# A two-block transformer kernel: the second mixer's attention regrouped into units of four heads, with half of the output mix placed between them

## The reference

```python
# first block, one layer
mix = (jax.nn.sigmoid(gate_a) * (nsa_out @ w_proj_a[layer])
       + jax.nn.sigmoid(gate_b) * (ret_out @ w_proj_b[layer]))
...
# second mixer, fox branch: 8 heads of 64, causal, with a forget term F per head
s = jnp.einsum('bqhd,bkhd->bhqk', qb, k) * scale
s = s + Fq[..., None] - F[:, :, None, :]
s = jnp.where(mask[None, None], s, -jnp.inf)
p = jax.nn.softmax(s, axis=-1)
...
# second mixer, dsa branch: an index score picks 128 keys of each query
score = jnp.einsum('bqh,bqhk->bqk', iwb, jax.nn.relu(dots))
_, sel = lax.top_k(score, top_k)
...
merged = jax.nn.sigmoid(ga) * (ya @ w_br_fox) + jax.nn.sigmoid(gb) * (yb @ w_br_dsa)
return merged @ w_out
```

## Time and profile before

| what | us |
|---|---|
| median of 3 runs | 2283.05 (2280.05 to 2284.55) |
| the profiled execution, its own time | 2287.16 |
| its span, first to last instruction | 2285.1 |
| PE busy | 2159.1 |
| DVE, ACT, POOL busy | 942.5, 768.4, 796.9 |

### The profile page before, as it was taken

How to read it: one execution, slowest core, us unless ns; L and a number is a source line. 1 busy time by engine, 2 the same in 40 slices (tenths; PEclk the granted TensorE clock), 3 DMA queues, 4 the chain that set the end, 5 groups by cost and what they waited for, 6 DMA issues and landing times.

```text
span 2285.1 us, 26992 instructions
## 1 busy us (share of the span) xinstructions
PE 2159.1 (94%) x9858; PEld 1684.8 (74%) x9858; DVE 942.5 (41%) x1403; ACT 768.4 (34%) x1321; POOL 796.9 (35%) x333
## 2 busy tenths in 40 slices
PE   5997799999999999799999989999899998999999
PEld 4777455587778888688788877745567887888887
DVE  6662544432662353546711136637842124110110
ACT  3332355533332332323232244334353224221221
POOL 2363311134354354234444423300002442444442
PEclk8998899999999999799999989958699999999999
DMA  5344111134567457336434422210002342334332
GB/s 137 97 117 106 27 47 38 32 83 111 138 175 207 125 157 209 103 101 176 124 84 100 102 71 68 67 26 1 1 1 56 84 110 65 93 100 105 88 92 74
DMA packets 156810, 211.22 MB, mean 92 GB/s; under 512 B 15240, under 2 KB 133416, under 8 KB 156584
## 3 DMA queue, kind: packets, MB, share of 16 engines
q1 hardware_dynamic: 140128, 166.24, 29.2%
q10 hardware_dynamic: 16584, 43.64, 6.3%
HBM read 206.69 MB, written 2.10 MB: 91 GB/s over the span
## 4 chain that ended last, share of the span: by engine, by line
PE 79%; DVE 9%; issue 6%; ACT 3%; POOL 2%; ACTq 1%; DMA 1%; DVEq 0%; POOLq 0%
PE ps L611 23%; PE ps L613 22%; PE ps L612 22%; PE ps L980 2%; POOL wlo L575 2%; PE ps L1002 2%; PE ps L1014 1%; PE ps L856 1%; PE ps L885 1%; DVE top L2092 1%; DVE score L2095 1%; PE ps L842 1%; PE ps L872 1%; DVE xT L2129 1%; PE ps L861 1%
## 5 line engine op out<-in xcount | busy, mean ns | idle before, releaser
L575 POOL TENSOR_TENSOR wlo<-raw,whi 128x1024 fp32r<-128x1024 f32 (+1 forms) x317 | 781.4, 2480 | 1443.4 <-ACT whi L1280 1426.2
L611 PE MATMUL ps<-hhi,whi 128*128 128x512 f32 x1488 | 596.9, 401 | 14.3 <-DVE hlo L1778 7.4
L613 PE MATMUL ps<-hhi,wlo 128*128 128x512 f32 x1488 | 585.3, 393 | 0.0
L612 PE MATMUL ps<-hlo,whi 128*128 128x512 f32 x1488 | 585.3, 393 | 0.0
L1280 ACT ACTIVATE whi<-raw 128x1024 fp32r<-128x1024 f32 x309 | 315.9, 1053 | 408.1 <-PE ps L613 401.8
L611 PEld LDWEIGHTS ps<-hhi,whi 128*128 128x128 f32 x1488 | 282.7, 190 | 86.7 <-issue 20.5
L613 PEld LDWEIGHTS ps<-hhi,wlo 128*128 128x128 f32 x1488 | 282.8, 190 | 60.2
L612 PEld LDWEIGHTS ps<-hlo,whi 128*128 128x128 f32 x1488 | 283.6, 191 | 56.7 <-issue 1.4
L611 PE MATMUL ps<-hidhi,whi 128*128 (+1 forms) x608 | 236.9, 390 | 3.0 <-DVE mod L2150 3.0
L613 PE MATMUL ps<-hidhi,wlo 128*128 (+1 forms) x608 | 236.6, 389 | 0.0
L612 PE MATMUL ps<-hidlo,whi 128*128 (+1 forms) x608 | 236.5, 389 | 0.0
(11 more groups left out here) (324 smaller groups left out, 2743.3 us busy)
## 6 DMA issues: line engine op xcount, KB each, us to landing
raw<-in_ffn_w SPq DMA_DIRECT2D x264, 256.0 KB, 3.8
raw<-in_w_in SPq DMA_DIRECT2D x154, 256.0 KB, 4.0
trig<-in_ada_w ACTq DMA_DIRECT2D x72, 512.0 KB, 4.3
raw<-in_w_up SPq DMA_DIRECT2D x64, 256.0 KB, 3.9
raw<-in_w_down SPq DMA_DIRECT2D x64, 256.0 KB, 3.8
raw<-in_w_out SPq DMA_DIRECT2D x32, 256.0 KB, 3.7
xrow<-in_x ACTq DMA_DIRECT2D x2, 1024.0 KB, 10.0
raw<-in_cmp_k_w SPq DMA_DIRECT2D x8, 256.0 KB, 3.9
```

Source lines behind the costliest of these rows:

```text
L575: last = pool.tensor_tensor(lo, src, hi.bitcast(F32), ALU.subtract)
L611: pe.matmul(out_, lhi, rhi, start=first, stop=False)
L612: pe.matmul(out_, lhi, rlo, start=False, stop=False)
L613: return pe.matmul(out_, llo, rhi, start=False, stop=last)
```

## The change

Four things are rebuilt. (1) fox and dsa become 16 units of four heads (`UNITS2`: fox blocks 3, 3, 2, 2, 1, 1, 0, 0, then dsa 0, 0, 1, 1, 2, 2, 3, 3) in 18 rounds, in the form of `nsa_attention`: paired scores, all masks and the forget term added by PE (the forget row `FThl` in two fp32r parts on 8 + 8 partitions, picked by `selr`), maxima straight from PSUM, one `normalise` per unit, `transpose` in place of a product with a diagonal. The index products become 10 units of two or four heads, blocks 1, 2, 3, on two PSUM banks, and the selection runs in the order 1, 2, 3 by the table `SELECTED`. (2) The fox branch of the output mix (`mixa2`, 12 slabs) runs in rounds 8 to 16 by the table `FILL2`; the dsa branch (`mixb2`, 12 slabs) follows the attention. (3) The gates of the interleaved branches are Tanh of half the input in place of Sigmoid; the branch sum is taken with (1 + tanh), and halved later. (4) The first norm squares rows of x (`xrow`, now loaded in four tiles of 128 whole rows) on ACT with accumulation along the row; constants are loaded in three pieces; SP's slabs from the second on wait for x; ACT rounds slab 0 between the squares, slab 1 after the vectors, and slabs 2 and 3 after the `hhi` chunks.

```diff
+        UNITS2 = [("fox", i, cc) for i in reversed(range(NT)) for cc in range(2)]
+        UNITS2 += [("dsa", i, cc) for i in range(NT) for cc in range(2)]
+        BLOCKS2 = [i + 1 for _, i, _ in UNITS2]
+        TURNS2 = [sum(BLOCKS2[:u]) for u in range(len(UNITS2) + 1)]
+        FILL2 = [0] * 9 + [2, 4, 7, 10, 13, 16, 19, 22, 24, 24]
...
-        SELECT_AT = [(12, 21), (22, 28), (28, 34)]
...
+        SELECTED = [0, 0, 4, 12, 20, 27, 34, 40, 46, 57, 68, 78, 88, 96, 102, 102, 102, 102, 102]
...
+                if s == 1:
+                    for t in range(NT):
+                        sp.wait_ge(ld_x[t], 16)
...
-            def attention(ph):
-                steps = STEPS[ph]
-
-                def scores(s):
-                    t = steps[s]
-                    n, i = t["n"], t["i"]
-                    if s >= 3:
-                        pe.wait_ge(at_exp[ph], s - 2)
-                    mask = {"causal": (i * P, C_CAUSAL, P), "fox": (i * P, C_CAUSAL, P), "cmp": (0, C_CMP + 32 * i, n),
-                            "dsa": None}[t["mask"]]
-                    mm = pe.matmul(ps[:, s % 3, 0:n], t["q"], t["k"], start=True, stop=mask is None)
-                    if mask is not None:
-                        at, c, w = mask
-                        mm = pe.matmul(ps[:, s % 3, at:at + w], ident, cst[:, c:c + w], start=False, stop=True)
-                    mm.then_inc(at_qk[ph], 1)
...
-                def turn(s):
-
-                    t = steps[s]
-                    pe.wait_ge(at_nrm[ph], s + 1)
-                    if s >= 2:
-                        pe.wait_ge(at_pt[ph], s - 1)
-                    for j in range(len(t["v"])):
-                        nk = min(P, t["n"] - j * P)
-                        mm = pe.matmul(ps[0:nk, 3 + s % 2, j * P:j * P + P], PB4[s % 4][:, j * P:j * P + nk], diag[:, s % 2, :],
-                                       start=True, stop=True)
-                    mm.then_inc(at_tr[ph], 1)
...
+            def fd_attention():
+
+                def score_pair(u, p):
+                    kind, i, cc = UNITS2[u]
+                    n, c, x = (i + 1) * P, 2 * cc + p, 4 * u + 2 * p
+                    if x >= 2:
+                        pe.wait_ge(at_exp["fd"], x - 1)
+                    for g in range(2):
+                        rows_ = slice(64 * g, 64 * g + 64)
+                        q, k = (fqT, fkT[rows_, c, 0:n]) if kind == "fox" else (dqT, dkT[rows_, 0, 0:n])
+                        pe.matmul(ps[:, (x + g) % 3, 0:n], q[rows_, c, i * P:(i + 1) * P], k, start=True, stop=False)
+                    if x == 0:
+                        pe.wait_ge(f_ready, 1)
+                    if kind == "dsa" and cc == 0 and p == 0:
+                        pe.wait_ge(ix_sel, i + 1)
+                    for g in range(2):
+                        bank = ps[:, (x + g) % 3, :]
+                        if kind == "fox":
+                            h = 2 * c + g
+                            pe.matmul(bank[:, 0:n], selr[:, h:h + 1].broadcast_to([P, P]), FThl[:, 0:n], start=False,
+                                      stop=False)
+                            mm = pe.matmul(bank[:, i * P:n], cstr[:, 0, :], cstr[:, 1, :], start=False, stop=True)
+                        else:
+                            mm = pe.matmul(bank[:, 0:n], cstr[:, 0, :], sel[:, i, 0:n], start=False, stop=True)
+                        mm.then_inc(at_qk["fd"], 1)
...
+                    for p in range(2):
+                        for g in range(2):
+                            mm = pe.transpose(ps[:, 3 + t % 2, (2 * g + p) * P:(2 * g + p + 1) * P],
+                                              P3[u % 3][:, 2 * p + g, j * P:j * P + P], ident)
+                    mm.then_inc(at_tr["fd"], 1)
...
+                    if kind == "fox":
+                        for p in range(2):
+                            for g in range(2):
+                                c = 2 * cc + p
+                                v = fv[:, j, 64 * (2 * c + g):64 * (2 * c + g) + 64]
+                                mm = pe.matmul(ps[64 * g:64 * g + 64, 5, P * c:P * c + P], v,
+                                               SQ[t % 4][:, P * (2 * g + p):P * (2 * g + p) + P], start=j == 0 and p == 0,
+                                               stop=j == i, skip_group_check=True)
+                    else:
+                        for g in range(2):
+                            mm = pe.matmul(ps[64 * g:64 * g + 64, 5, 256 * cc:256 * cc + 256], dvrow[:, j, :],
+                                           SQ[t % 4][:, 256 * g:256 * g + 256], start=j == 0, stop=j == i)
+                    mm.then_inc(at_pv["fd"], 1)
+
+                def filler(r, a, b):
+                    for q in range(4 * FILL2[r] + a, 4 * FILL2[r] + b):
+                        branch("mixa2", q // 4, q % 4, q % 4 + 1, O2["a"], (at_done["fd"], NT))
+
+                n = len(UNITS2)
+                for r in range(n + 2):
+                    nb = BLOCKS2[r - 2] if r >= 2 else 0
...
+                    for j in range(nb + 1):
+                        if j == (nb + 1) // 2:
+                            if 2 * r + 1 < len(UNITS):
+                                index_unit(2 * r + 1)
+                            if r < n:
+                                score_pair(r, 1)
+                        if j < nb:
+                            turn(r - 2, j)
+                        filler(r, quarters * j // (nb + 1), quarters * (j + 1) // (nb + 1))
+                        if j >= 1:
+                            values(r - 2, j - 1)
...
                 if n == 0:
+                    sc.wait_ge(ld_misc, 16)
+                    sc.activation(early[:, 0:1], col(C_EPS), ACT.Sqrt)
+                    for t in range(NT):
+                        if t == 2:
+                            high(0)
+                        sc.wait_ge(ld_x[t], 16)
+                        sc.activation((st, tmp)[t // 2][:, 2 * (t % 2):2 * (t % 2) + 2, :].rearrange("p a n -> p (a n)"), xrow[:, t, :],
+                                      ACT.Square, accum_out=early[:, 1 + t:2 + t]).then_inc(x_summed, 1)
+                    sc.wait_ge(x_summed, NT)
+                    sc.activation(root[:, 0, :], early[:, 1:1 + NT], ACT.Sqrt, bias=col(C_EPS), scale=1.0 / D).then_inc(n_root, 1)
+                    for m in (7, 6, 5, 4):
+                        sc.wait_ge(x_turned, KD - m)
+                        sc.activation(xT[:, m, :], ps[:, m, :], ACT.Copy).then_inc(x_ready, 1)
                     sc.wait_ge(vec_turned, 1)
                     sc.activation(vec[:, :], ps[:, 2, 0:P], ACT.Copy).then_inc(vec_ready, 1)
                     sc.wait_ge(vec_turned, 2)
                     sc.activation(vec2[:, :], ps[:, 3, 0:V2_N], ACT.Copy).then_inc(vec_ready, 1)
...
-                        if r % 6 == 3:
-                            for c in range(2):
-                                sc.wait_ge(*one_done(mb_g, "mixb1", r // 6, c, 2))
-                                if r >= 6:
-                                    sc.wait_ge(mb_m, 2 * (r // 6 - 1) + c + 1)
-                                sc.activation(gsig[:, c, :], ps[:, 6 + c, :], ACT.Sigmoid).then_inc(mb_sig, 1)
+                        if r % 6 in (2, 3):
+                            c = r % 6 - 2
+                            sc.wait_ge(*one_done(mb_g, "mixb1", r // 6, c, 2))
+                            if r >= 6:
+                                sc.wait_ge(mb_m, 2 * (r // 6 - 1) + c + 1)
+                            sc.activation(gsig[:, c, :], ps[:, 6 + c, :], ACT.Tanh, scale=0.5).then_inc(mb_sig, 1)
...
+                def filled(r):
+                    for d in range(FILL2[r], FILL2[r + 1]):
+                        n, step, c = d // 6, d % 6 // 2, d % 2
+                        if c == 1:
+                            high(AT["mixa2"] + d // 2 + SLOTS)
+                        if step == 1:
+                            sc.wait_ge(*one_done(mb_g, "mixa2", n, c, 2))
+                            if n >= 1:
+                                sc.wait_ge(mb_m, 8 + 2 * (n - 1) + c + 1)
+                            sc.activation(gsig2[:, c, :], ps[:, 6 + c, :], ACT.Tanh, scale=0.5).then_inc(mb_sig, 1)
...
-            for half in range(2):
-                cols = slice(half * D // 2, (half + 1) * D // 2)
-                sc.dma_start(xrow[:, :, cols], T["x"][0].rearrange("(t p) d -> p t d", p=P)[:, :, cols])\
-                  .then_inc(ld_x[half], 16)
+            sc.dma_start(cst[:, 0:C_HD128], T["consts"][:, 0:C_HD128]).then_inc(ld_cst, 16)
+            for t in range(NT):
+                sc.dma_start(xrow[:, t, :], T["x"][0, t * P:(t + 1) * P, :]).then_inc(ld_x[t], 16)
+            with nc.allow_non_contiguous_dma(reason="9 narrow columns"):
+                sc.dma_start(cst[:, C_MISC:C_END], T["consts"][:, C_MISC:C_END]).then_inc(ld_misc, 16)
...
+            def fd_attention():
+
+                def maxima(u, p):
...
```

(30 more changed lines are left out.)

656 lines of the change are left out of this document (254 added, 402 removed), and 2 rows, old and new, of the table C_END.

## The result

The changed kernel took 2157.7 us (median of 4 runs, 2156.4 to 2160.5) against 2283.8 us before (4 runs): a ratio of 0.945, 95% interval 0.943 to 0.947. The forecast was 2166. The profiled execution took 2156.66 us, its span is 2154.6.

What follows compares the result with a forecast made beforehand. PE, busy 2159.1 of 2285.1 us, was taken as the bound. Gains of 99.7 (attention), 6 (gates) and 11 (start), 116.7 off 2287.2, gave 2170.5; 2166 after allowing for that execution lying 4.1 above the median; range 2140 to 2202.

Steps and rivals of the forecast that it cites:

- the likeliest case: Whole kernel: full clock in fox rounds 2 to 4 and from round 8 on; 2166 us, chance 0.48.
- rival B: Second mixer's attention: clock stays full in the fox part, 12 us less, 2154 us; chance 0.17.
- the fox term: Rounds 0 to 7 of the second mixer's attention: 70 us with losses plus 12 for the clock, 82 us.
- the clock: Fox rounds 0, 1 and 5 to 7 at half clock because PE waits there: 11.4 us, 12 with the 5%.
- the larger engine of each round: Rounds 0 to 17: the longer of PE and DVE summed, 66.7 and 113.5 us, plus 5% for losses.
- fox values: Fox rounds, PE: four products of 128 columns per block, taken at 0.80 us, between 0.58 and 1.01.
- Rival A: Fox part stays at half clock to round 7, PE the longer, 104 us against 82: 2188 us; chance 0.22.
- Dsa rounds: Rounds 8 to 17, with the fox branch's twelve slabs: 113.5 us plus 5%, 119 to 119.5 us.
- the collision: DVE and POOL excluding each other in rounds 8 to 16: 1 to 3 us, inside the 5%.
- Gates: First mixer's attention: no table loads at four gates, PE's waits shrink; gain 6 us, from 0 to 8.
- Start: First norm: first product at 26 instead of 37.41, gain 11 us, from 6 to 15.
- Slabs 2 and 3: Start: ACT rounds them at about 37, POOL finishes slab 2 at 40, when PE wants it; possibly late.

Runs made afterwards that it cites:

- the second profile: The changed kernel run again unaltered, on the same chip as the run with sums later: 2161.2 us, ratio to before 0.946.
- the entry wait: Against the changed kernel, PE waits for one ACT copy of 2048 columns before the first matmul behind the second projection: 2170.6 us (one run).

## Why the prediction was right, and where not

**Which case came.** The time, 2157.7, lies between the likeliest case (2166) and rival B (2154). The mechanism of the likeliest was right: scores at half the cost per head, the fox branch between the dsa units at full clock, half clock in a part of the fox rounds. What was mis-sized is the fox term, 82 us where 72.0 were measured, which is 10 of the 11.7 us by which the section came out shorter. Within it the clock is the term that failed, 12 us for about 2. No run takes the pairing of heads, the fox branch between the rounds and the masks on PE apart, so their shares of the 111 us rest on the forecast's sum coming out, and not on an experiment; why the clock holds in the new form, worth up to 43 us, stays open.

**Fox rounds.** The sum was 66.7 (the larger engine of each round) + 5% = 70, and 12 for the clock. The 70 agree with the estimate of about 70 at full clock, but in part by luck. PE's own part was right: 52 forecast, 51.5 at full clock. Inside it fox values for a block were taken at 0.80; they cost 0.58 from start to start (1507.31 to 1507.89), the lower end, so other groups cost 4 us more than I gave them. DVE's part was 60.4 for 65. With the measured loads the larger engines add up to about 63 us, so the loss beside them is 11% and not 5%: two errors of 4 us that cancel. "I add the larger of the two in each round" is right for the longer stretch of rounds 5 to 7 (with DVE's work left out they become 4.7 us shorter, at like clock) and wrong for rounds 2 to 4, where leaving out a third of DVE's work made rounds 3 and 4 shorter by 0.3 us each. What stands there is a ring: scores, maxima, exponentials, copies, values, next scores. Its waits show at the values or at the scores, depending on ACT's order.

**The clock.** Twelve us were added for half clock in rounds 0, 1 and 5 to 7. Rounds 0, 1 and 5 stayed at full clock, and with them 9 of the 11.4 us; that is the step that failed. For rounds 6 and 7 the forecast was 0.7 and 1.7, and they took 7.30 and 7.70 us where the second profile has 6.84 and 6.97: there the rule, that half clock costs only what PE exceeds the longer engine by, came out. A part of round 2 was not on the list. PE's busy time rose by 7.2 us in all, but most of that filled waits. That the clock falls where PE waits was right in kind: a wait of 4.25 us at the entry was followed by 13.7 us of half clock. But which wait sets it off isn't fixed: behind the same 2.2 us in round 1 came 0, 3.4, 6.8 or 13.7 us of half clock in different runs, and the unaltered kernel had 17.1 us from round 6 on in one profile and 6.8 from the end of round 7 in another. Rival A, half clock up to round 7, didn't happen in any of thirteen profiles. Its ground, the 64.5 us in the earlier trace rows, I can't explain: neither the wait ahead of it nor a thin load does, since the entry wait was undone in 13.7 us by rounds of the new form. The Trainium skill (TensorE: Matmul & The Clock Gate, Part 1) holds that sustained work releases the clock. The new rounds agree with it (full clock again after 3.4 to 20.5 us), the old steps with PE busy 64.5 of 64.5 us at 0.51 don't; what it is between them that matters was not tried and stays open.

**Dsa rounds.** 119.5 forecast, 117.8 measured; PE busy 114.4, idle 3.4. 3.0 of these are one wait in round 10 for `foxlo`. DVE there, and the two passes of POOL beside it:

```profile
1554.37 2.39 POOL L534 TENSOR_TENSOR wlo<-raw,whi 128x1024 fp32r<-128x1024 f32 x1 [78.54 <-ACT whi L1223]
1555.10 2.33 DVE L1956 TENSOR_SCALAR trig<-trig,rcpg 128x128 f32<-128x128 f32 x4
1563.08 2.35 POOL L534 TENSOR_TENSOR wlo<-raw,whi 128x1024 fp32r<-128x1024 f32 x1 [6.32 <-ACT whi L1223]
1563.99 1.66 DVE L2050 TENSOR_SCALAR sel<-score 128x384 fp32r<-128x384 f32 x1
1565.57 0.68 DVE L1963 TENSOR_TENSOR foxlo<-ps,foxhi 128x512 fp32r<-128x512 f32 x1
```

Four scalings of 128 columns take 0.9 us elsewhere, from the first's start to the last's end, here 2.33; the mask took 1.66, where one of 512 columns takes 0.43, and ended after POOL's slab. That is the collision forecast at 1 to 3 us, and it is about 2.7. I had placed it in rounds where PE is the longer; the mask was not on my list, and it stood directly ahead of the one result that PE needed. By the Trainium skill (SBUF — State Buffer, Who interferes with whom) a DVE instruction in a mode with two ports and one of GpSimd exclude each other for a whole instruction. Both cases fit that: each time DVE was through 0.2 to 0.7 us after POOL.

**Gates.** 6 forecast with 8 as the upper end, 8.6 measured. PE's waits in that stage fell from 10.4 to 2.3 us. I had counted the waits at the gates of the earlier trace rows and not those of the values behind them, which the loads also delayed.

**Start.** Forecast 26 for the first product and 11 us; the trace:

```profile
16.73 0.30 ACT L1247 ACTIVATE root<-early,cst 128x4 f32<-128x4 f32 x1
24.73 0.77 PE L570 MATMUL ps<-hhi,whi 128*128 128x512 f32 x1 [2.53 <-DVE hlo L1739]
34.08 5.05 POOL L534 TENSOR_TENSOR wlo<-raw,whi 128x512 fp32r<-128x512 f32 x4 [10.04 <-ACT whi L1221]
```

ACT began at 10.01 (10.5 forecast), the root stood at 16.73 (18). Slabs 2 and 3, feared for 37 to 40, were rounded by ACT from 32.9 on and by POOL by 39.1, and PE did not wait for them. The 1.6 us given back up to the attention are the clock's: of the twelve other profiles eight took 224.7 to 225.4 us for this stretch and four 226.3 to 226.7, the kernel before 225.1; this one has 3.4 us at half clock (222.7 to 226.1) that none of the eight has. Of the 2.4 us lost at the end of the program, 0.95 are a new wait of PE ahead of `out2` and 1.5 are PE's busy time, with 13.7 us of half clock there for 10.2.

**The rest of what was to be seen.** Entry and dsa branch: 2.5 and 65.5 forecast, 2.48 and 65.50 measured; `out2` starts behind one wait of 0.95 us and runs on. DVE over 90% busy in rounds 1 to 4: 96, 92, 83 and 90. PE over 90% from round 10: so from round 11, but 81% in round 10 with its wait; its idle time in rounds 8 to 17 is 3.4 us (wrong from 10). PEclk 1.00 after round 8 but for 3.4 us in round 10, behind that wait. The first mixer's attention was to take 170 to 176 us in place of 180. The 180.0 us of the earlier trace rows end 8.4 us before the stage does; between the instructions of the 179.42 us above there were 188.0:

```profile
276.41:464.39 187.98, 177.31 (x985) 109.26 (x985) 86.31 (x248) 100.07 (x266) 28.59 (x12) 1.00 0.15 35
```

So it is 8.6 us shorter, where 4 to 10 were forecast, with one table load, at its first exponential.

## What to carry to other kernels

Adding the longer engine of each round gives a fair length, but not the cause. Before calling an engine the bound of a stage with hand-overs, leave part of its work out and compare round by round, and only rounds at like clock: slower matmuls fill the waits, so that the sum of PE's idle time hid here that DVE's work set the pace of some rounds and not of others. Run the same kernel twice before a pattern of the clock is put down to an edit; here it moved between rounds 2 and 6 with no change. Where waits go from one product to the next, look at all waits of the busiest engine together and try edits together: 13.3 us of idle time became 8.3 with less half clock. And work that can go anywhere (here the index units) belongs in rounds in which PE has least to do.

## What the hardware showed

The kernel before spent 233 us of its span at half clock; the thirteen profiles of the new forms 117 to 160, and two of the same kernel 137 and 140, with different places in the fox rounds. The same round of the same kernel took 7.30 us at a granted clock of 0.56 and 6.84 at 1.00, with PE busy 6.91 and 4.26 us. A mask that DVE writes in 0.43 us for 512 columns took 1.66 for 384 beside a POOL pass. And a table load of 1.28 us inside a chain that PE follows cost 0.8 to 1.1 us of the whole time.
